# Mixture-of-experts steps of one 64-row pair and two 32-row chunks in place of two 64-row chunks, in a two-layer diffusion kernel

## The reference, cut to what matters

```python
def moe(h, router_w, router_b, w_gate, w_up, w_down):      # 16 experts, D_EXPERT = 256
    scores = sigmoid(t @ router_w)                         # t: 640 x 1024
    # one group of 4 experts is chosen per token, and the top 2 experts in it
    ...
    a = einsum('td,edf->tef', t, w_gate)
    b = einsum('td,edf->tef', t, w_up)
    act = silu(a) * b * gates[:, :, None]
    return einsum('tef,efd->td', act, w_down)
```

## Time and profile before

| | us |
|---|---|
| median of 3 runs | 1113.89 |
| lowest, highest | 1113.77, 1116.4 |
| profiled execution, span | 1112.5 |
| its own time outside the profile | not given apart; the span is 1.4 below the median |

### The profile page before, as it was taken

One profiled execution on the slowest core, in us unless ns is written; L12 is line 12 of the kernel. 1 busy time (PEld: TensorE's weight loads), 2 busy tenths in 40 slices (PEclk: granted clock), 3 DMA queues, 4 the chain that ended last, 5 costly groups with the idle time before them and its releaser, 6 DMA issues.

```text
span 1112.5 us, 17990 instructions
## 1 busy us (share of the span) xinstructions
PE 1058.8 (95%) x5918; PEld 589.1 (53%) x5919; DVE 572.7 (51%) x1223; ACT 389.0 (35%) x800; POOL 204.8 (18%) x313
## 2 busy tenths in 40 slices
PE   3999999999999899999999999899999979999996
PEld 0566564555544455555546655555644445555552
DVE  0334545665345754454574545476724674534557
ACT  0332224444211244444333222454511134444540
POOL 0133456000000100100152435800000011001003
PEclk9999999999999999999999999999999999999999
DMA  9940006668801799999981000557540379999917
GB/s 351 361 138 1 1 9 238 217 222 302 331 19 40 248 378 377 381 358 366 332 289 41 1 1 0 187 194 279 207 149 38 112 260 376 381 379 380 376 78 284
DMA packets 129064, 241.47 MB, mean 217 GB/s; under 512 B 12304, under 2 KB 92192, under 8 KB 122864
## 3 DMA queue, kind: packets, MB, share of 16 engines
q1 hardware_dynamic: 115904, 194.83, 50.1%
q0 software_dynamic: 7056, 25.69, 6.3%
q10 hardware_dynamic: 6048, 20.22, 4.5%
HBM read 213.63 MB, written 27.10 MB: 216 GB/s over the span
## 4 chain that ended last, share of the span: by engine, by line
PE 80%; DMA 8%; DVE 3%; issue 3%; SPq 3%; POOL 1%; ACT 1%; DVEq 0%; POOLq 0%; ACTq 0%
PE bank L1120 17%; PE pair L1045 12%; PE pair L1160 9%; PE pair L762 7%; PE pair L777 6%; DMA big<-ada_w 4%; PE pair L895 4%; PE pair L794 3%; PE bank L811 3%; PE bank L931 3%; PE bank L672 3%; PE pair L1090 3%; PE bank L910 2%; PE bank L746 2%; DMA big<-y_rows,big 2%
## 5 line engine op out<-in xcount | busy, mean ns | idle before, releaser
L1120 PE MATMUL bank<-big,actT 128*64 (+1 forms) x928 | 206.3, 380 | 2.4 <-ACT actT L1445 1.9
L1120 PE MATMUL bank<-actT 128*64 128x256 f32 x928 | 206.5, 381 | 0.0
L1120 PEld LDWEIGHTS bank<-big,actT 128*64 128x64 f32 x928 | 124.7, 137 | 83.1 <-issue 26.0
L1045 PE MATMUL pair<-big,actT 128*128 128x512 f32 x320 | 142.7, 598 | 0.0
L1120 PEld LDWEIGHTS bank<-actT 128*64 128x64 f32 x928 | 124.7, 137 | 0.0
L1160 PE MATMUL pair<-big 128*64 (+1 forms) x464 | 106.0, 598 | 0.7 <-ACT big L1470 0.7
L1045 PEld LDWEIGHTS pair<-big,actT 128*128 128x128 f32 x320 | 59.0, 190 | 67.8 <-issue 67.6
L762 PE MATMUL pair<-big,actT 128*128 128x384 f32 (+1 forms) x320 | 93.6, 447 | 0.3 <-ACT actT L1218 0.2
L1988 DVE TENSOR_REDUCE mx<-pair 128x1 f32<-128x640 f32 x64 | 52.7, 823 | 72.0 <-PE pair L896 71.9
L1642 POOL DMA_INDIRECT big<-h_rows,big x29 | 27.7, 956 | 304.3 <-PE pair L1090 286.9
L762 PEld LDWEIGHTS pair<-big,actT 128*128 128x128 f32 x320 | 59.5, 190 | 29.3 <-ACT actT L1218 1.9
(11 more groups left out here) (274 smaller groups left out, 1628.9 us busy)
## 6 DMA issues: line engine op xcount, KB each, us to landing
big<-ada_w SPq DMA_DIRECT2D x48, 1024.0 KB, 5.0
big<-w_gate SPq DMA_DIRECT2D x32, 1024.0 KB, 13.1
big<-w_up SPq DMA_DIRECT2D x32, 1024.0 KB, 16.3
big<-w_down SPq DMA_DIRECT2D x32, 1024.0 KB, 14.5
y_rows<-big ACTq DMA_DIRECT2D x28, 512.0 KB
big<-w_out SPq DMA_DIRECT2D x4, 2048.0 KB, 13.4
big<-mod_rows SPq DMA_DIRECT2D x16, 512.0 KB, 9.2
h_rows<-big ACTq DMA_DIRECT2D x10, 512.0 KB, 2.7
```

What stands on the lines that cost most here:

```text
L1045: m = mm(dst, actT[:, k, t * P:(t + 1) * P], vw.wo[n][:, k, :], start=(k == order[0]), stop=(k == order[-1]))
L1120: m = mm(dst[CH * h:CH * h + CH, 0:DE], xgT[:, k, CH * h:CH * h + CH], weights(h, k * 2 * DE + lo, DE), start=(k == 0), stop=(k == DC - 1) ...
```

## The change

It sets `CH = 32`. A step is then four chunks, which are run as three tiles: 64, 32 and 32 slots. The first tile is a pair of chunks of one expert; the slots of some chunks are moved (by `shift`, `tail`, `moved`) so that this holds in each step, and each odd expert has at least two chunks, expert 0 four. Step 0 is then all expert 0, and runs as one tile of 128 without copies. The ring's order of places is 1, 2, 3, 0, 4; expert 3 (place 0) is loaded once the second norm is done, and SP issues each load behind the landing of the same matrix of the expert before, so that three semaphores count all loads in expert order. Gate and up are read as rows of 8 contiguous k-slices for each partition (8 KB runs); the rows of the second norm are written in the matching order (`by_row` and `plain`: element p * 8 + k goes to k * 128 + p). ACT now copies all of the second tile's weights and DVE all of the third's, in six pieces of 1024 columns each, with three buffers in turn; PE uses the weights piece by piece (k-slices 0 to 3 and 4 to 7 of gate, the same of up, and the two k-slices of down), and counts `used` after each. The list of rows is made by PE behind the first piece of step 0, no longer ahead of it.

```diff
-CH = 64
-NSTEP = 18
+CH = 32
+NSTEP = 19
+TILES = [(0, 64), (64, 32), (96, 32)]
+PLACES = (1, 2, 3, 0, 4)
...
                 def load_expert(e):
...
-                    sp.dma_start(wgu[s][:, :, 0:DE], w_gate[l, e].rearrange("(k p) n -> p k n", p=P)).then_inc(ld_w[s], 16)
+                    if e > 0:
+                        sp.wait_ge(ld_wg, landed(l, e - 1))
+                    sp.dma_start(wg[s], w_gate[l, e].rearrange("(p k) n -> p (k n)", k=DC)).then_inc(ld_wg, 16)
...
                 load_expert(2)
                 sp.wait_ge(op_x, L(op_x) + 2 * NT)
+                sp.wait_ge(h_ready, L(h_ready) + 2 * NT)
+                load_expert(3)
                 sp.wait_ge(r_gate, L(r_gate) + 1)
                 sp.wait_ge(r_slot, L(r_slot) + 1)
-                load_expert(3)
                 load_expert(4)
...
-                for j in range(2 * NT):
...
-                stay_awake(a7, 2)
+                stay_awake(a7, 3)
...
+                def products(n, land, place, first):
+                    tiles = [(0, P)] if first else TILES
+                    pe.wait_ge(b_ta, n + 1)
+                    pe.wait_ge(b_td, n + 1)
+                    for i in range(4):
+                        if first and i == 1:
+                            list_rows()
+                        weights = weights_of(n, i, land, place, first)
+                        dst = (tb4, tb5)[i // 2]
+                        for k in range(4 * (i % 2), 4 * (i % 2) + 4):
+                            for c, (lo, m_) in enumerate(tiles):
+                                m = mm(dst[lo:lo + m_, 0:DE], xgT[:, k, lo:lo + m_], weights(c, k % 4 * DE, DE),
+                                       start=(k == 0), stop=(k == DC - 1), tile_position=(0, lo), skip_group_check=True)
+                        m.then_inc(used, 1)
...
-                            for h in range(2):
-                                m = mm(pair[1][CH * h:CH * h + CH, j * HALF:(j + 1) * HALF], acT[:, k, CH * h:CH * h + CH],
+                            for c, (lo, m_) in enumerate(tiles):
+                                m = mm(pair[1][lo:lo + m_, j * HALF:(j + 1) * HALF], acT[:, k, lo:lo + m_],
...
+                def part_copy_w(n, part, i):
+                    land, slot = part
+                    if i % 2 == 0:
+                        act.wait_ge((ld_wg, ld_wu, ld_wd)[i // 2], land)
+                    act.wait_ge(used, used_at(n, i - 3))
+                    f(parts[1][i % 3], slot[:, i * PIECE:(i + 1) * PIECE], ACT.Copy).then_inc(w_a, 1)
+                def step(n, first, last):
+                    if not first:
+                        part = part_place(n)
+                        part_copy_w(n, part, 3)
+                    act.wait_ge(used, used_at(n, 1))
                     f(sil, tb4[:, 0:DE], ACT.Silu).then_inc(b_sil, 1)
+                    if not first:
+                        part_copy_w(n, part, 4)
+                        part_copy_w(n, part, 5)
...
+                    rows_copy(n + 2)
+                    part = part_place(n + 1)
+                    for i in range(3):
+                        part_copy_w(n + 1, part, i)
                     act.wait_ge(b_yd, n + 2)
                     act.dma_start(y_rows[bass.ds(n * P, P), :], yb).then_inc(b_st, 16)
+                step(0, True, False)
-                with act.Fori(0, n_more) as i:
+                with act.Fori(1, n_more) as i:
...
-                            reached(gu_mm, n_steps * 2)
-                        if i == (2 if l == 0 else 6):
-                            reached(dn_mm, n_steps)
+                            reached(used, used_in(n_steps, 3))
+                        if i == 2 and l == 0:
+                            reached(used, used_in(n_steps, 5))
...
-                    link(v.scalar_tensor_tensor(xn[t % 2], x[:, t, :], rs[:, NT + t:NT + t + 1], vw.G[:, c2, :], ALU.mult,
-                                                ALU.mult))
+                    h2 = by_row(xn[t % 2])
+                    link(v.scalar_tensor_tensor(h2, plain(x[:, t, :]), rs[:, NT + t:NT + t + 1], plain(vw.G[:, c2, :]),
+                                                ALU.mult, ALU.mult))
```

More of the change, by code:

```diff
@@ L393, in step_kernel @@
         mod_st = sem("mod_st")
-        ld_w = [sem(f"ld_w{s}") for s in range(RING)]
+        ld_wg, ld_wu, ld_wd = sem("ld_wg"), sem("ld_wu"), sem("ld_wd")
         y_fill = sem("y_fill")
@@ L1107, in products @@
[L1107 to L1123 removed]
+                    land = pe.value_load(eland[0:1, bass.ds(n, 1)], min_val=16, max_val=landed(DEPTH - 1, NE - 1))
@@ L1139, in turn_act, with rest @@
+                def rest(n, land, place, first, last):
+                    tiles = [(0, P)] if first else TILES
                     def turn_act(k):
@@ L1170, in _ @@
                 n_more = pe.value_load(n_more_s[0:1, 0:1], min_val=NSTEP_MIN - 1, max_val=NSTEP - 1)
-                rest(0, False, weights)
+                rest(0, land_0, place_0, True, False)
                 def step(n, last):
-                    rest(n, last, products(n))
+                    land, place = load_place(n)
+                    products(n, land, place, False)
+                    rest(n, land, place, False, last)
                 with pe.Fori(1, n_more) as i:
@@ L2132, in _ @@
                         v.memset(startx[:, 0:1], 0.0)
+                        v.memset(single[:, 0:1], 0.0)
                     if j == 6:
@@ L2258, in early_tables, with step @@
                     m.then_inc(e_hot, 1)
-                def step(n, last):
+                def step(n, first, last):
                     if last:
                         early_tables()
+                    if not first:
+                        part = part_place(n)
+                        for i in range(3, NPIECES):
+                            part_copy_w(n, part, i)
                     ve.wait_ge(b_sil, n + 1)
-                    ve.wait_ge(gu_mm, n * 2 + 2)
+                    ve.wait_ge(used, used_at(n, 3))
                     for k in range(2):
@@ L2279, in step @@
                         link(add_early(l, 0, 0))
-                    ve.wait_ge(dn_mm, n + 1)
                     if not last:
-                        down().then_inc(w_d, 1)
+                        part_copy_w(n + 1, part, 1)
+                    ve.wait_ge(used, used_at(n, 5))
                     ve.wait_ge(b_sel, n * 2 + 2)
@@ L2289, in step @@
                     tt(yb, pair[1][:, :], yb, ALU.mult).then_inc(b_yd, 1)
-                with ve.Fori(0, n_more) as i:
-                    step(i, False)
-                step(n_more, True)
+                    part_copy_w(n + 1, part, 2)
+                step(0, True, False)
+                with ve.Fori(1, n_more) as i:
+                    step(i, False, False)
+                step(n_more, False, True)
             l = DEPTH - 1
```

329 lines of the change are left out of this document (176 added, 153 removed).

## The result

The changed kernel takes 1433.7 us (median of 4, 1433.56 to 1435.19) against 1115.0 (median of 4, 1113.77 to 1116.4): a ratio of 1.285, 95% interval 1.283 to 1.288. The forecast was 1079, with a range from 1060 to 1175. What came is rival (b) of the prediction in its full form, priced there at 1407: tiles of unlike size take turns.

What follows compares the result with a forecast made beforehand. TensorE was taken to bound the expert loops at 12.12 us a step. Terms -48.5 + 8 + 1 + 6 + 1 - 2.4 = -35 took the span from 1112.5 to 1077.5 us, median 1079, range 1060 to 1175.

Steps and rivals of the forecast that it cites:

- rival (b): Gate, up and down, 23 steps: unlike tiles take turns, 1407 us, chance 0.15; or overlap with gaps only, 1171, chance 0.08.
- Three tiles in a window: Expert products: tiles of 64, 32 and 32 run side by side, adding 0.
- Fewer steps: Expert loops: 25 steps where there were 29, at 12.12 us each, -48.5 us.
- TensorE's queue and copies: Loop steps: queue 0.2 us, piece 3's copy on ACT 0.15, together 0.35 x 23 = +8 us (0 to 20).
- The table load: ACT's 1.28 us table load, 27 times in the expert loop, should go.
- Loads: Expert weights in 8 KB runs: about 405 GB/s, cost 0 (0 to 6 per layer); y_rows gathers may meet w_in, +1.
- Rival (c): Expert loops: loads bound them, rate stays at 380, 6 us per layer, 1091 us; chance 0.05.
- Routing and the first step: Step 0: routing hidden, gather 1 issued later, so down starts 3 us later; +6 us for two layers (0 to 10).
- Second norm: Norm ahead of routing: writes with a stride of 128 elements, 0 to 2.6 us per layer, taken as +1.
- The end: Behind the last steps: DVE's L2289 1.3 us earlier and POOL's wait gone, -2.4 us (0 to -2.6).

Runs made afterwards that it cites:

- e5: Changed kernel with four equal tiles of 32, a step's rows turned by 64 so every product is kept: 1097.4 us, ratio 0.983.
- e1: Changed kernel with the 64-slot tile split in two of 32, one reading the second source's weights (those rows' values wrong): 1097.8 us, ratio 0.983.
- e6: e5 with ACT's copy of piece 3 put ahead of its store and the value loads behind it: 1084.7 us, ratio 0.973.
- e3: Kernel before with both chunks run as two tiles of 32 each, four equal tiles (some rows' output wrong): 1130.3 us, ratio 1.014.
- e9: e5 with the edits of e6 and e8 together: 1087.2 us, ratio 0.974.
- e2: Kernel before with only its second chunk's products split, giving tiles of 64, 32 and 32: 1561.7 us, measured once.
- e10: e9 with w_gate and w_up loaded in 1 KB runs again and the second norm written in plain order: 1102.7 us.
- e7: e5 with the list of rows made before step 0's products and copied ahead of DVE's long comparison and sum: 1097.3 us.
- e8: e5 with DVE's tables for the last rows spread between its copies of pieces 3 to 5 in the last step: 1091.2 us, ratio 0.977.

## Why the prediction was wrong

*Three tiles in a window*, taken at 0, is the step that failed; the runs show 15.3 us per step in its place (27.42 less 12.12). The sentence was "in all rows a tile in other columns costs nothing", and every such row had tiles of one size. The one row with two sizes showed weights held back and a gap; the prediction saw it and put it down to columns that overlapped. Rival (b) had the mechanism and nearly the size: 14.3 us per step against 15.3 measured, 0.10 per change against 0.139, 1407 against 1433.7. What was wrong was the chance. The Trainium skill (TensorEngine Tiling (Array Packing), Key Properties) says that a change of the tiling mode drains the engine; the trace agrees, for tiles of 64 and of 32 columns that share no column, and gives the price of a change, 0.139 us, beside the turns.

*Fewer steps*: 25, as counted. At 27.42 us each that is no gain; at 12.6, in e5, it is.

The other terms can be read in e1 and e5, which don't pay for the sizes: 1097.4 against 1079, 18 us more.

*TensorE's queue and copies*: together +8 (0.35 per step). The mechanism was right and the size too small, by the value loads of more than 0.28 us that the earlier trace rows didn't have. e1's period is 12.59 us ((1053.63 less 927.71) / 10), 0.47 more than before, and e6 shows that the copy of piece 3 is worth 12.8 us by itself, 0.55 per step where 0.15 was put. Without it the period is below that of before, so the queue costs nothing there; in e3, with the old pieces, it goes with the 0.4. The table load left the loop, as expected.

*Loads*: right. 8 KB runs reach 411 to 420 GB/s in e9's fullest slices, and no load holds the loop for long (2.2 us of TensorE's idle time in e9). The time to landing of `w_gate`, 7.4 us where it was 13.1, shows nothing of the runs: with 1 KB runs and slow steps, in e2, it is 5.8. Rival (c)'s price, 6 us per layer at 380, is 12 for two; e10 measured 15.5 at 361 to 384.

*Routing and the first step*: gather 1 was issued 3 us later, as put (layer 0: 394.91 against 387.26, the mask 381.21 against 376.61). But e7 shows that such a gain or loss is not passed on one to one, for the granted clock moves with the wait. From the out-projection to down of step 0, e1 took 5.0 us more in layer 1, against 3.5 put; 1.1 of them is TensorE's turn of the rows at a granted clock of 0.50 (2.40 us, 911.32 to 913.72, where it was 1.31), and down itself is another 0.8 longer. The prediction had no term for the clock.

*Second norm*: +1 put for both layers. The two pieces behind the last product are 0.36 us (L1829, 1052 against 688 ns) and 0.70 us (L2190, 1986 against 1286) longer, in each layer, so about 2 for both. The prediction took the plain row as nearest; the strided form is 1.6 times as long. The Trainium skill (SBUF — State Buffer, the note on cachelines) says that accesses which cross into new lines pay; the trace agrees with its direction, at 2016 against 1278 ns.

*The end*: -2.4 was wrong in sign. From the last loop step's down to the end e1 takes 41.4 us, before it was 37.1, since DVE's tables stood ahead of three copies that the last step had not had (and the granted clock fell to 0.52 behind that wait). e8 takes 37.3, so it got this back. The prediction asked what DVE does sooner, not what the last step now has queued behind the tables.

*The start*: no term of the change. In the kernel after the out-projection begins 3.9 us later than before (its group of 3.63 us at 302.08 against 298.18), with a load of `norm_g` on the chain. One might blame expert 0's loads in 8 KB runs beside it, but that load is as long in e2, which has 1 KB runs:

```profile
283.58 15.50 DMA big<-norm_g
...
285.48 14.32 DMA big<-norm_g
```

(the kernel after, then e2.) And in e1, with 8 KB runs, the group begins at 297.90. Of the 3.9 us, 2.6 were there before that load was waited for: TensorE began the last products for `ada_w` at 276.25 us, before the change at 273.63. What the other 1.3 are the runs don't show.

Not tried by themselves: the order of the ring's places, and expert 3 behind the second norm.

## What to carry to other kernels

Here products in different columns of the array overlapped only while their tiles had one size, 64 or 32. Before a layout with chunks of several sizes, look for a row in which the sizes stand in one window; if there is none, price the turn in full, or cut the large tile to the small one's size. Where a row shows a thing once and an explanation makes it harmless (the gap in the earlier trace rows), the explanation needs a row too.

A gain in a wait ahead of TensorE must be read with the granted clock behind it, and two edits that each pay alone are to be timed together.

## What the runs showed of the hardware

- A change between tiles of 64 and 32 columns costs 0.139 us, and tiles of the two sizes don't run together even in disjoint columns (18.11 against 7.1 us for the same 16 slices). Between 2 x 64 and 4 x 32 there is no difference (7.13 and 7.10 us).
- A still time of TensorE is not always followed by the lower clock: e6_copy3 stands still for 3.51 us (to 1053.43) and is granted 1.00 behind it, e9_both for 2.68 (to 1052.03) and is granted 0.54. What tells them apart is open.
- A value load of ACT takes 0.27 to 0.30 us in the kernel before, e2 and e3, and 0.27 to 1.11 us in e1 (median 0.28); in the kernel after the longest is 1.49. What makes them long is open.
- DVE writing 1024 elements with a stride of 128 elements: 2016 against 1278 ns; reading one input with it too: 1967 against 1224.
